# Wide matmuls over both halves of an operand, a token layout for the last phase, and a new order of the setup, in a two-block transformer kernel

## The reference

```python
h = rmsnorm(x, ln1)
hq, hk, hv, hr, ha, hatt, hgate = split(h @ w_in)
o = gla_mixer(hq, hk, hv, log_a)                       # (S, H, dv)
o = o * rsqrt(mean(o * o, -1) + EPS)                   # over the 256 of a head
o = o * gla_gn * silu(hr);  y_gla = o @ w_o_gla
logits = q @ k.T * hd ** -0.5 + bias                   # per group and head, masked
y_att = softmax_over_groups(...) @ w_o_attn
x = x + (sigmoid(g_gla) * y_gla + sigmoid(g_att) * y_att) @ w_out
x = x + square(relu(rmsnorm(x, ln2) @ w_mlp1)) @ w_mlp2
x = x + sigmoid(rmsnorm(x, ln3) @ w_pg) * (p @ w_pp)
x = rmsnorm(x, ln_f)
for i in range(2):                                     # second block
    h = h + 0.5 * swiglu_ffn(rmsnorm(h, ffn_norm1[i]), ffn1[i])      # 1024 -> 2816 -> 1024
    h = h + (conv_module if i == 0 else mla)(rmsnorm(h, mix_norm[i]))
    h = h + 0.5 * swiglu_ffn(rmsnorm(h, ffn_norm2[i]), ffn2[i])
return rmsnorm(h, final_norm)
```

## Time and profile before

| | us |
|---|---|
| median of 3 runs (lowest, highest) | 1612.07 (1611.82, 1613.92) |
| the profiled execution | 1612.46 |
| its span, first to last instruction | 1610.7 |
| TensorE busy | 1552.0 (96%) |
| DVE busy | 1077.2 (67%) |
| ScalarE busy | 664.9 (41%) |
| GpSimd busy | 110.5 (7%) |
| DMA, mean over the span | 161 GB/s |

### The profile page before, as it was taken

One profiled execution on the slowest core, in us unless ns is written; L12 is line 12 of the kernel. 1 busy time (PEld: TensorE's weight loads), 2 busy tenths in 40 slices (PEclk: granted clock), 3 DMA queues, 4 the chain that ended last, 5 costly groups with the idle time before them and its releaser, 6 DMA issues.

```text
span 1610.7 us, 30625 instructions
## 1 busy us (share of the span) xinstructions
PE 1552.0 (96%) x12779; PEld 1515.0 (94%) x12779; DVE 1077.2 (67%) x1339; ACT 664.9 (41%) x815; POOL 110.5 (7%) x127
## 2 busy tenths in 40 slices
PE   5999999999999989999997999999999999999995
PEld 3999999999999989999986999999999997999995
DVE  5766655579875579666785866567665687866653
ACT  2624336434333345444543534345343434434341
POOL 2000000003000014000031100000000100100000
PEclk8999999999999989999999999999999999999997
DMA  5544664355655546655632666566665643466451
GB/s 155 172 136 137 184 182 146 105 171 181 184 184 183 181 136 177 182 162 170 207 118 66 177 181 184 157 185 203 182 176 163 197 131 106 141 182 183 152 183 50
DMA packets 268213, 259.85 MB, mean 161 GB/s; under 512 B 15622, under 2 KB 267092, under 8 KB 268106
## 3 DMA queue, kind: packets, MB, share of 16 engines
q1 hardware_dynamic: 267034, 256.33, 53.1%
q0 software_dynamic: 1072, 1.98, 0.5%
HBM read 257.21 MB, written 1.07 MB: 160 GB/s over the span
## 4 chain that ended last, share of the span: by engine, by line
PE 58%; DVE 3%; issue 2%; ACT 0%; POOL 0%; POOLq 0%; DVEq 0%; ACTq 0%
PE ps L547 54%; PE misc L734 2%; PE misc L683 1%; DVE rstd L1097 1%; PE misc L572 1%; PE misc L582 0%; DVE parts L1079 0%; DVE wsplit L1061 0%; PE ps L709 0%; DVE plain L1445 0%; POOL acc L1562 0%; PE misc L687 0%; DVE plain L1448 0%; PE ps L704 0%; ACT root L894 0%
## 5 line engine op out<-in xcount | busy, mean ns | idle before, releaser
L547 PE MATMUL ps<-xa,wsplit 128*128 128x256 f32 x7104 | 871.0, 285 | 9.8 <-DVE xa L1079 5.8
L547 PEld LDWEIGHTS ps<-xa,wsplit 128*128 128x128 f32 x7104 | 862.3, 193 | 15.6 <-DVE xa L1079 6.8
L1061 DVE TENSOR_TENSOR wsplit<-raw,wsplit 128x1024 fp32r<-128x1024 f32 (+2 forms) x532 | 593.1, 1143 | 134.8 <-ACT wsplit L851 118.2
L851 ACT CAST wsplit<-raw 128x1024 fp32r<-128x1024 f32 (+2 forms) x532 | 500.6, 968 | 402.8 <-DMA raw<-in_ffn_w_dram 176.2
L547 PE MATMUL ps<-parts,wsplit 128*128 128x256 f32 x3984 | 485.9, 285 | 13.2 <-DVE parts L1090 9.0
L547 PEld LDWEIGHTS ps<-parts,wsplit 128*128 128x128 f32 x3984 | 483.1, 193 | 14.8 <-issue 8.2
L909 ACT ACTIVATE work<-t 128x512 f32<-128x512 f32 x48 | 30.4, 633 | 221.8 <-DVE t L1142 221.8
L1166 DVE TENSOR_TENSOR work<-ps,work 128x512 f32<-128x512 f32 x44 | 30.4, 691 | 76.5 <-PE ps L547 75.2
L887 ACT ACTIVATE sq<-x 128x512 f32<-128x512 f32 x40 | 25.1, 632 | 123.5 <-DVE x L1195 71.4
L1562 POOL TENSOR_TENSOR acc<-acc,sq 128x512 f32<-128x512 f32 x36 | 51.2, 1421 | 317.1 <-ACT sq L887 292.1
L1559 POOL COPY acc<-sq 128x512 f32<-128x512 f32 x14 | 9.8, 702 | 904.4 <-ACT sq L887 879.4
(11 more groups left out here) (212 smaller groups left out, 669.4 us busy)
## 6 DMA issues: line engine op xcount, KB each, us to landing
raw<-in_ffn_w_dram SPq DMA_DIRECT2D x176, 512.0 KB, 3.7
raw<-in_w_in_dram SPq DMA_DIRECT2D x76, 512.0 KB, 3.7
raw<-in_ffn_w_dram SPq DMA_DIRECT2D x96, 384.0 KB, 3.1
raw<-in_w_mlp_dram SPq DMA_DIRECT2D x64, 512.0 KB, 3.6
raw<-in_conv_w_pw_dram SPq DMA_DIRECT2D x24, 512.0 KB, 3.5
raw<-in_ffn_w_dram SPq DMA_DIRECT2D x32, 256.0 KB, 3.0
raw<-in_w_o_gla_dram SPq DMA_DIRECT2D x8, 512.0 KB, 3.4
raw<-in_w_out_dram SPq DMA_DIRECT2D x8, 512.0 KB, 4.4
```

Of the source, the lines that this page charges most:

```text
L547: last = mm(o, still, moves, start=st and n == 0, stop=en and n == 2, skip_group_check=True)
L851: nc.scalar.copy(wsplit[:, slot, 0:kn, 0, 0:p.width], raw[:, slot, 0:kn, 1, 0:p.width]).then_inc(hi_done, 1)
L1061: TT(wsplit[:, slot, 0:kn, 1, 0:p.width], raw[:, slot, 0:kn, 1, 0:p.width], wsplit[:, slot, 0:kn, 0, 0:p.width].bitcast(F32), ALU.subtract ...
```

## The change

- In the phases named in `WIDE`, all groups but a phase's last (and the last too where the sums are only kept) have two matmuls per product: the high weight piece with both halves of the activations, 512 columns, into the whole bank, and the low piece with the high half, 256 columns, into the upper half of the bank. ScalarE copies the upper half to `lohalf` (`take_lohalf`), and DVE adds it to the lower half into `val` and frees the bank; then it evacuates from there.
- `split_gained` multiplies into a buffer of its own (`gained`), and then splits it with one cast and one subtraction.
- The last phase, ffn2's second down phase, has layout "T". x is transposed to tokens behind the groups 18 and 19 of the up phase before it, the squares are summed per token by ScalarE, and the final factor is one number per partition. Four transfers write the output.
- The linear attention's outputs are made by token, squared and summed by ScalarE, scaled by DVE, and transposed.
- The bias is added to the logits by DVE, with a reversed access to `sbias`, and not by TensorE.
- At the start x is SP's first transfer; the gains and the setup data are issued by ScalarE. TensorE waits for `ident_ready`, transposes gains and x, and makes the relative bias behind gla_q's first group. ScalarE copies x out of PSUM. The angles move to att_k2 and att_v2.

The diff, cut to its core:

```diff
+WIDE = (["gla_q", "gla_k", "gla_v", "mlp1", "mlp2"] + [f"att_{w}{g}" for w in "qkv" for g in range(3)]
+        + [f"ffn{n}_{w}{i}" for n in (1, 2) for w in ("up", "down") for i in range(2)])
 
...
+    def halves(self, g):
+
+        return self.name in WIDE and (g < self.groups - 1 or self.evac[0] in ("keep", "keep_tok"))
...
+        def bias_of(h, t):
+
+            b = sbias[:, h % 2, :, :]
+            return bass.AP(b.tensor, b.offset + (t + 1) * P - 1, [list(b.ap[0]), [T, ATT_G], [-1, (t + 1) * P]])
...
-            sp.dma_start(ropec[:, :], a["rope_c"]).then_inc(s_setup, 16)
-            sp.dma_start(posi, a["positions_2"][0].partition_broadcast(P)).then_inc(s_setup, 16)
-            sp.dma_start(onehot, a["bias_c"].rearrange("b g j -> b (g j)")).then_inc(s_setup, 16)
-            sp.dma_start(relrow[0:REL_BUCKETS, :], a["rel_bias"]).then_inc(s_setup, 16)
...
+                if p.name == "w_o" and g == 3 and j == 0:
+                    sp.wait_ge(used, by["uq_nope"].block0)
+                    sp.dma_start(gain_row, a["final_norm_2"].partition_broadcast(P)).then_inc(s_gain_row, 16)
...
+                            if p.halves(g):
+                                still, both = (wh, mov) if F else (mh, wboth)
+                                mm(o, still, both.rearrange("p h t -> p (h t)"), start=st, stop=False,
+                                   skip_group_check=True)
+                                still, moves = (wl, mh) if F else (ml, wh)
+                                last = mm(o[:, T:2 * T], still, moves, start=False, stop=en, skip_group_check=True)
                             else:
-                                terms = [(mov[:, m, c * P:(c + 1) * P], wboth[:, w, :]) for w, m in
-                                         ((0, 0), (1, 0), (0, 1))]
-                            for n, (still, moves) in enumerate(terms):
-                                last = mm(o, still, moves, start=st and n == 0, stop=en and n == 2,
-                                          skip_group_check=True)
+                                terms = [(wh, mh), (wh, ml), (wl, mh)] if F else [(mh, wh), (ml, wh), (mh, wl)]
+                                for n, (still, moves) in enumerate(terms):
+                                    last = mm(o[:, 0:T], still, moves, start=st and n == 0, stop=en and n == 2,
+                                              skip_group_check=True)
                     last.then_inc(used, 1)
...
 
-            pe.wait_ge(const_ready, 1)
+            pe.wait_ge(ident_ready, 1)
...
-            pe.wait_ge(s_setup, 16 * 6)
-            for g in range(ATT_G):
-                last = mm(ps[0:ATT_H, 1, g % 2, 0:BIAS_N] if g < 2 else misc[0:ATT_H, 3, 0:BIAS_N],
-                          relrow[:, g * ATT_H:(g + 1) * ATT_H], onehot[:, g * BIAS_N:(g + 1) * BIAS_N],
-                          start=True, stop=True)
-            last.then_inc(s_pe, 1)
...
                     dv_did(pe, "st2")
+                    for t in range(NT):
+                        for h in range(GLA_H):
+                            at = t * D + h * GLA_DV
+                            mm(misc_flat[:, at:at + GLA_DV], flat(44, 4)[:, (h * NT + t) * P:(h * NT + t + 1) * P],
+                               plain[:, 8 + 2 * h + t, :], start=True, stop=False, skip_group_check=True)
+                            for n in range(max(1, 2 * t), 2 * t + 2):
+                                r = (n % 2) * GLA_CHUNK
+                                last = mm(misc_flat[r:r + GLA_CHUNK, at:at + GLA_DV],
+                                          plain[:, h, n * GLA_CHUNK:(n + 1) * GLA_CHUNK],
+                                          plain[:, 52 + (n - 1) * GLA_H + h, :],
+                                          start=False, stop=True, skip_group_check=True)
...
+                if k == "oT":
+                    dv_did(pe, "on1")
...
                             for t in range(NT):
...
-                                          start=False, stop=(n == 3), skip_group_check=True)
...
-                                last = mm(o, flip[:, :], bias[:, g, (1 - t) * P:T], start=False, stop=True,
                                           skip_group_check=True)
                     last.then_inc(s_pe, 1)
...
+            def tokens_of_x(t):
+
+                if t == 0:
+                    pe.wait_ge(new_x, new_x_at["ffn2_up1"] + 4)
+                for k in range(NC):
+                    last = transpose_to(misc_flat[:, t * D + k * P:t * D + (k + 1) * P], x[:, k, t * P:(t + 1) * P])
+                last.then_inc(s_pe, 1)
...
+            def take_lohalf(p, g, i, per):
+
+                G = p.group0 + g
+                act.wait_ge(used, lin(p.block(g, len(p.kns) - 1) + 1, RING if i is not None else 0, i))
+                if G >= 2:
+                    act.wait_ge(val_done, lin(G - 1, per, i))
+                nc.scalar.copy(lohalf[:, G % 2, :, :], ps[:, G % 2, :, T:2 * T]).then_inc(lohalf_done, 1)
...
+                if kind == "out":
+                    for t in range(NT):
+                        act.wait_ge(new_tok, 2 * g + t + 1)
+                        act_fn(sq[:, g % 2, t, :], x_tok[:, t, g * W:(g + 1) * W], ACT.Square,
+                               accum_out=sum_tok[:, t, g:g + 1]).then_inc(squared_tok, 1)
...
+                    for n in range(8):
+                        last = act_fn(unit(n), misc_flat[:, n * GLA_DV:(n + 1) * GLA_DV], ACT.Square,
+                                      accum_out=stat[:, n:n + 1])
+                    last.then_inc(s_ac, 1)
...
+            act.dma_start(wa2[0:GLA_RANK, :], a["w_a2"][0]).then_inc(s_setup, 16)
+            act.dma_start(wa2[GLA_RANK:GLA_RANK + 1, :], a["b_a"]).then_inc(s_setup, 16)
+            act.dma_start(relrow[0:REL_BUCKETS, :], a["rel_bias"]).then_inc(s_setup, 16)
+            act.dma_start(onehot, a["bias_c"].rearrange("b g j -> b (g j)")).then_inc(s_setup, 16)
+            act.dma_start(ropec[:, :], a["rope_c"]).then_inc(s_setup, 16)
+            act.dma_start(posi, a["positions_2"][0].partition_broadcast(P)).then_inc(s_setup, 16)
...
+            for c in range(4):
+                pe_did(act, f"xT{c}")
+                nc.scalar.copy(x[:, 2 * c:2 * c + 2, :], misc[:, c, :].rearrange("p (k t) -> p k t", k=2)
+                               ).then_inc(new_x, 1)
...
-                    ins = TS(dst[:, c, 0, :], src[:, c, :], gain[:, at + c:at + c + 1], None, ALU.mult)
+                    ins = TS(gained[:, c, :], src[:, c, :], gain[:, at + c:at + c + 1], None, ALU.mult)
                 step(ins)
-                for c in range(n):
-                    STT(dst[:, c, 1, :], src[:, c, :], gain[:, at + c:at + c + 1], dst[:, c, 0, :].bitcast(F32),
-                        ALU.mult, ALU.subtract).then_inc(ready, 1)
-                halves[0] += n
+                split(dst, gained[:, :, :], n)
...
+                if p.halves(g):
+                    v.wait_ge(lohalf_done, lin(p.low0 + g + 1, per, i))
+                    after_split()
+                    TT(val[:, :, :], total, lohalf[:, G % 2, :, :], ALU.add).then_inc(val_done, 1)
+                    v.wait_ge(val_done, lin(G + 1, per, i))
+                    total = val[:, :, :]
...
+                    if p.halves(g):
+                        step(STT(t2[:, :, :], total, 0.0, total, ALU.max, ALU.mult))
+                    else:
...
+                        step(TS(half_tok[:, :], rstd_tok[:, :], 0.5, None, ALU.mult))
+                    at = slice(g * W, (g + 1) * W)
+                    for t in range(NT):
+                        STT(x_tok[:, t, at], total[:, t, :], half_tok[:, t:t + 1], x_tok[:, t, at], ALU.mult, ALU.add
+                            ).then_inc(new_tok, 1)
+                    v.wait_ge(new_tok, 2 * g + 2)
...
                     if p.name == "mlp2" or "_down" in p.name:
...
+                if k in ("on0", "on1"):
+                    t = int(k[2])
+                    if t == 0:
                         ac_did(v, "oroot")
-                    step(vec.reciprocal(unit(8 + h), unit(8 + h)))
...
+                    for h in range(GLA_H):
+                        n = 4 * t + h
+                        ins = TS(unit(24 + n), misc_flat[:, n * GLA_DV:(n + 1) * GLA_DV], stat[:, 16 + n:17 + n], None,
+                                 ALU.mult)
...
+                        TT(three(l0), three(o0), bias_of(h, 0), ALU.add)
+                        step(TT(three(l1), three(o1), bias_of(h, 1), ALU.add))
+                        o0, o1 = l0, l1
...
+            v.wait_ge(squared_tok, 8)
+            done("outsum", vec.tensor_reduce(half_tok[:, :], sum_tok[:, :, :], AX_X, ALU.add))
+            ac_did(v, "outroot")
+            done("out", vec.reciprocal(rstd_tok[:, :], root_tok[:, :]))
+            for h in range(2):
+                part = out_tok[:, 0, h * D // 2:(h + 1) * D // 2]
+                TS(part, part, rstd_tok[:, 0:1], None, ALU.mult).then_inc(scaled_dve, 1)
```

294 lines of the change are left out of this document (161 added, 133 removed), and 2 rows, old and new, of the table GLA_AT.

## The result

The kernel after took 1586.58 us (median of 5 runs, 1582.06 to 1595.81) against 1612.07 us (1610.96 to 1613.92) on the same chip: ratio 0.9844, 95% interval 0.9829 to 0.9859. It is faster by 25.5 us, where 86.8 were forecast, and lies outside the range of 1511 to 1558.

A forecast was written before the change was run, and what follows sets the result against it. TensorE's stream of weight-product matmuls was taken as the bound, 1394 of 1610.7 us. The terms sum to -86.8 us, from 1612.46 to a forecast of 1525.5 us; the eight-in-ten range was 1511 to 1558.

The forecast's parts named there:

- The wide products: In 2720 weight products, a 512-column and a 256-column matmul would take 0.336 us instead of 0.360: -65.3 us.
- the 13 ns: Step of a 256-column weight-product matmul, 0.120 us, above its 0.107 us of streaming; read as the weight load.
- Rival 1: In the wide products the 13 ns are a price per instruction: -35 instead of -65, 1555 us; chance 12%.
- What wide products add: Low-half copies on ScalarE and additions on DVE in up phases, mlp1, gla_v and first groups: +2.0 us (0 to 8).
- Input first: At the start, x and gains land by about 8.5 us, so the first norm sums end at 24.5, not 37.58: -13.1 us.
- The relative bias behind gla_q's first group: Moved from the start, six records of 384 columns at 0.32 us each at full clock: +1.9 us.
- Split with gain: In w_pp, multiplication, cast and subtraction shorten the chain TensorE waits for, three groups: -1.4 us; elsewhere hidden.
- Token layout of the last phase: At the end, 9.0 us behind the last product instead of 22.6: -13.6 us (-11 to -15).
- The transposes in ffn2_up1: Price of the last phase's token layout: sixteen transposes and eight one-column norm records at 0.112 us, +2.7 us.
- The recurrence by token: In the linear attention's outputs, TensorE does 2.0 us less but waits about 2 us before transposes: 0 (-2 to +2).
- Bias by DVE: In gates, 7.9 us of matmuls leave TensorE, but the wait for the softmax takes the gain: 0 (-4 to +3).

The follow-up runs named there:

- p2: The kernel before with nothing but the wide products (and the low halves' copies and additions); 1600.43 us, ratio 0.9917.
- p1: The changed kernel with an empty list of wide phases, all else as changed; 1598.20 us, ratio 0.9911.
- s1: b1 with the gain rows ahead of the weights at the start, and x transposed before the gain rows; 1564.16 us, ratio 0.9702.
- e1: The changed kernel with the split with gain as it was in the kernel before; 1577.10 us, ratio 0.9771.
- after again: The changed kernel once more, unchanged, for a second profile; 1588.12 us, ratio 0.9836.
- b1: The changed kernel with the old split with gain and the order wide, wide, narrow, narrow; 1568.28 us, ratio 0.9735.
- e2: The changed kernel with the order wide, wide, narrow, narrow in each k-chunk; 1578.38 us, ratio 0.9791.
- c1: s1 with GpSimd's first five sets of convolution weights made some ten weight blocks later, in ffn1_up0; 1560.91 us, ratio 0.9676.
- c2: c1 with wide and narrow matmuls in turn, as in the change; 1571.57 us, ratio 0.9744.
- c3: c1 without any wide product, three matmuls of 256 columns in each; 1587.67 us, ratio 0.9847.

## Why the prediction was wrong

- **The wide products: wrong, and 51 of the 61 us of the miss.** The step that failed is that the 13 ns belong to the weight load and "with long streaming it disappears", which I took over from plain fp32 to rounded operands. Measured: 13.3 to 13.7 ns per fp32r matmul with 128 stationary columns at any width from 256 to 512 columns (what they are stays open: with 64 stationary columns the step shrinks at 256 moving columns and grows at 512), and in turn up to 6 ns more per pair: 0.353 instead of 0.336. The term is 2720 x 0.007 = -19 by the steps instead of -65.3. With the half-clock stretch in ukv_v (+5.4 us in p2) p2 measured -12.1. Rival 1, a price per instruction, was the right one and had 12%; what I held against it were rows of plain fp32, and those do not price rounded operands. Its time of 1555 us was still too low: of the 31 us that it misses, the slower rhythm is some 16 (2720 x 0.006), the split with gain some 11 and the start 3.7, an estimate from the items here.
- **What wide products add (+2.0):** right in the pieces (0.586 and 0.691 us; DVE 97.1 of 125.7 us in ffn2_up0) and in mlp1 (92.07 against 93.01 us, no wait). The one wait on val_done is at the head of ffn1_up0, from GpSimd.
- **Input first (-13.1):** the mechanism was right, two sizes were wrong. The gain rows landed at 10.4 instead of 8.5 us, and DVE needed 12.3 us instead of 10.4 for the four splits and two rests, because GpSimd's additions from 17.06 to 21.70 us lie beside them (two multiplications 1.63 us instead of 0.62, a cast 1.38 instead of 0.43). The first full group starts at 28.2 (p1 29.1), -8.5 to -9.4; my own terms, 20.5 + 1.0 + 3.3, made 24.8 and not 24.5. s1 shows what held the rows up: the weights on SP's queue, by 3 us. The relative bias behind gla_q's first group took 2.0 us in p1, as forecast (1.9); the groups around it grew by 0.2 to 0.4 us only, since the granted clock there was at 2.4 GHz, and in before at 1.2 until 41.8 us.
- **Split with gain (-1.4):** wrong in sign. p1's stretches give +5.4 us (without pw1, which e1 has longer too: 87.9 against 86.3 us in before), e1 some 10 us beside wide products (5 to 18 by the intervals of e1 and after, 0 to 21 by those of e1 and after again), and b1 against e2 10 again. The new subtraction was priced from rows with GpSimd idle, the old pair from one with GpSimd at work.
- **Token layout of the last phase (-13.6):** right: 8.3 us behind the last product instead of 9.0, so -14.3. The transposes in ffn2_up1 (+2.7): +3.0 in p1.
- **The recurrence by token (0):** att_v2 went from 14.96 to 12.98 us, as the 2.0 fewer say, and att_k2 was 0.4 to 0.7 longer: about -1, inside the bounds.
- **Bias by DVE (0):** as forecast, the transposes start as soon as DVE's scaling ends, and TensorE waits for it:
```profile
292.48 0.62 DVE L1400 TENSOR_SCALAR logit<-logit,stat 128x768 f32<-128x768 f32 x1
...
293.15 1.20 PE L611 MATMUL misc<-ident,logit 128*128 128x128 f32 x9 [1.10 <-DVE logit L1400]
```
gates took 71.78 us instead of 74.01 (73.33 in p1): -0.7 to -2.2, inside -4 to +3.

The misses add up: 51.2 in the wide products (p2: -12.1 instead of -63.3) and 9.2 in the rest (p1: -14.3 instead of -23.5), 60.4 of the 61.3 us.

## What to carry to other kernels

Before a change that makes an instruction longer to save its fixed price, measure that price in a stream of the same operand type at two widths; a stream of another type has another price. Before a DVE instruction with two SBUF inputs replaces one on a chain that TensorE waits for, look at what GpSimd does in those very microseconds: its additions and products turned 0.69 us into 1.6 to 2.8. And price the old instruction and the new one in the same company.

## What was unexpected

- An fp32r matmul with 128 stationary columns costs 13.3 to 13.7 ns above its columns at 256 to 512 columns, a bf16 one 2.5; with 64 stationary columns 256 moving ones take 113 ns instead of 120, but 512 take 230 instead of 227.
- Wide and narrow in turn settle at 0.347 or 0.353 us per pair, in the same phase of the same kernel now at one and now at the other; the order wide, wide, narrow, narrow holds 0.348 and made the kernel 10.7 us faster (c1 against c2).
- Kernels with wide and narrow in turn spread by 6 to 14 us between executions, e2 and b1 in the other order by 9 to 10, p1 and c3 without wide products by 2 and 6, before by 2 to 4 in four series and 8 in one. The time at half clock differs too (between 50 and 1560 us of the span 58 us in after's profile, 48 in its second, 27 in before's). Whether it makes the spread, and what decides it, stays open.
- One DVE instruction can wait 66.6 us behind a row of GpSimd memsets.
